# Tile addresses at multiples of 128 bytes, and three-pass products that run from the last column to the first

## The chip, the cores and the metric

The kernel runs on one core of one Trainium2 chip. The time is device microseconds of one execution of the whole program; the number used is the median of the runs shown. Names of engines: PE is TensorE (matrix products), PEld its weight load, DVE VectorE, ACT ScalarE, POOL GpSimd, SP the queue that issues most of the DMAs.

## What is computed

Two blocks of a model on 512 tokens of width 1024 (and 256 context tokens), all in float32. The matrix products that matter here are these, cut from the reference:

```python
z, xbc, dt_raw, q, f, v, g = _split(t @ w_in, IN_SIZES)            # first mixer, latent and context
...
return jnp.concatenate([ys, os_], axis=-1).astype(h.dtype) @ w_out
...
a, gate = jnp.split(t @ w1 + b1, 2, axis=-1)                       # conformer
u = dwconv1d(a * jax.nn.sigmoid(gate), dw_w, dw_b)
...
v, gate = jnp.split(t @ w_up, 2, axis=-1)                          # feed-forward, 1024 -> 2 x 2816
return (jax.nn.gelu(gate, approximate=False) * v) @ w_down         # 2816 -> 1024
...
proj = h @ w_in[l]                                                 # second block
x = x + jnp.concatenate([o_nsa, o_rw, o_moba], axis=-1) @ w_out[l]
x = x + _conv_glu(_rmsnorm(x, ffn_norm[l]), ffn_w_in[l], ...)
```

There are three feed-forward parts (two of the first block's form, one `_conv_glu`), and between them a chunked state-space scan, a gated linear recurrence, a 31-tap convolution, three kinds of attention and a delta-rule recurrence.

## The kernel before

Activations lie transposed: 128 features on the partitions, 512 tokens (256 for the context) along the row. A dense product walks over tiles of 128 output features; each tile is summed in one PSUM bank over the `kt` blocks of 128 input features (8, 22 or 16 of them).

For accuracy a float32 operand is split into two tiles of type float32r, a high and a low part, and each block is multiplied in three passes by the helper `three_passes`: weights high with activations high (line 248), weights high with activations low (line 249), weights low with activations high (line 250). Each pass is one MATMUL whose moving operand, the one that streams through the array, is a 512-column row of activations, and one LDWEIGHTS of 128 columns of weights. Nearly all dense layers call this helper. The value projection (lines 441 to 443) and a part of the second block's projections (lines 3676 to 3678) write out three passes of their own, in which the weights are the moving operand; the 31 taps of the convolution (line 1277) and the scans are plain float32 products.

Weights come in by DMA on SP, are split into high and low by ACT and DVE one or two tiles ahead, and lie in rotating slots. The feed-forward layers use four slots: two in `pre_high` and `pre_low`, which belong to the core's fixed arena, and two in the layer's own `ffn_w_high` and `ffn_w_low`. PE works through the tiles in the written order; what releases it is the split (`low_done`), and a free bank (`banks_free`).

Each tile is a tensor allocated by the helpers `room`, `split_room` and `some_parts` of the class `Core` on a stack from the low end of the memory or, with `side="right"`, from the high end. Its address is whatever the stack stands at. Every allocation has the same address on all partitions, and each row of a tile is a multiple of 512 bytes long for the operands named here, so that all rows of a tile have the tile's own residue to 128 bytes. The residues in the built program:

| moving tile | residue | weight tile | residue |
|---|---|---|---|
| ffn_x_high, ffn_x_low | 0 | ffn_w_high, ffn_w_low | 0 |
| ffn_x_high, ffn_x_low | 0 | pre_high, pre_low | 96 |
| ffn_h_high, ffn_h_low | 96 | ffn_down_w_high, _low | 32 |
| ffn_h, conf_x, conf_in, mix_parts, h | 96 | pre_high, pre_low | 96 |
| conf_x_high, conf_x_low | 96 | conf_w_high, conf_w_low | 96 |
| conf_in, mix_parts | 96 | conf_out_w, out_w | 0 |
| h_high, h_low, h_ctx | 96 | f_w, q_w, gate_w, pj_w | 32 |
| h_high, h_low, h_ctx | 96 | xbc_w | 0 |
| y, o | 32 | mix_out_w | 64 |
| y, o | 32 | mix_first | 32 |
| v_w (moving) | 32 | h, h_ctx (as weights) | 96 |

Of the kernel before, what the change touches and what calls it, by code (L numbers as in the profile page):

```python
# [8 lines left out]
F32 = mybir.dt.float32  # L9
F32R = mybir.dt.float32r  # L10
# [5 lines left out]
P = 128  # L16
# [50 lines left out]
ALWAYS = len(CONST)  # L67
# [63 lines left out]


ARENA = 28 * 1024


class Core:


    def __init__(self, nc, ctx):
        self.nc = nc  # L140
        self.stages = self.rooms = 0
        self.banks = [ctx.enter_context(nc.psum_tensor(f"bank{i}", [P, SEQ], F32)) for i in range(8)]
        self.const_sb = ctx.enter_context(nc.sbuf_tensor("const_sb", [P, ALWAYS, P], F32))
        self.some = {}
        self.cols_sb = ctx.enter_context(nc.sbuf_tensor("cols_sb", [P, N_COLS], F32))
        ctx.enter_context(nc.sbuf_tensor("arena", [P, ARENA // 4], F32, side="right"))
        self.arena_at = nc.sbuf_top
        slab = DT * P * 4
        self.pre_ring = self.in_arena("pre_ring", [P, 2, DT, P], F32, 0)
        self.pre_high = self.in_arena("pre_high", [P, 2, DT, P], F32R, 2 * slab)  # L150
        self.pre_low = self.in_arena("pre_low", [P, 2, DT, P], F32R, 4 * slab)
        self.rstd = self.in_arena("rstd", [P, SEQ], F32, 6 * slab)
        self.mean = self.in_arena("mean", [P, SEQ], F32, 6 * slab + SEQ * 4)
        self.fold_sb = ctx.enter_context(nc.sbuf_tensor("fold_sb", [P, 4, DEPTH * 2 - 1, DT], F32))
# [33 lines left out]
    @contextmanager  # L188
    def room(self, side=None, **shapes):

        self.rooms += 1
        n = self.rooms
        with ExitStack() as ctx:
            yield [ctx.enter_context(self.nc.sbuf_tensor(f"{name}_{n}", shape, F32, side=side)) for name, shape in shapes.items()]

    @contextmanager
    def split_room(self, side=None, **shapes):

        self.rooms += 1
        n = self.rooms  # L200
        with ExitStack() as ctx:
            yield [tuple(ctx.enter_context(self.nc.sbuf_tensor(f"{name}_{part}_{n}", shape, F32R, side=side))
                         for part in ("high", "low")) for name, shape in shapes.items()]

    @contextmanager
# [8 lines left out]
    @contextmanager  # L214
    def some_parts(self, **shapes):

        self.rooms += 1
        n = self.rooms
        with ExitStack() as ctx:
            yield [ctx.enter_context(self.nc.sbuf_tensor(f"{name}_{n}", shape, F32R)) for name, shape in shapes.items()]  # L220

    @contextmanager
    def stage(self, *names):
# [21 lines left out]
def three_passes(pe, bank, weights, acts, start, stop):  # L245


    pe.matmul(bank, weights[0], acts[0], start=start, stop=False)  # L248
    pe.matmul(bank, weights[0], acts[1], start=False, stop=False)  # L249
    return pe.matmul(bank, weights[1], acts[0], start=False, stop=stop)  # L250


def fill(pe, core, bank, count):
# [14 lines left out]
def gemm(core, name, weights, acts, spans, out, tiles, unroll, bias=None, func=ACT.Identity, more=None,  # L268
# [19 lines left out]
    with core.room(**{f"{name}_ring": [P, rings, kt, P]}) as (ring,), \  # L288
# [60 lines left out]
        @block.tensor  # L349
        def _(pe):  # L350
            pe.sem_inc(tile_done, slots)
            with pe.Fori(0, steps) as i:
                for u in range(unroll):

                    pe.wait_ge(banks_free, i * unroll + u + 1)
                    for n in range(len(spans)):
                        for k in range(kt):
                            if n == 0 and k in (0, kt // 2):
                                pe.wait_ge(low_done, 2 * (i * unroll + u) + (k > 0) + 1)
                            mm = three_passes(pe, bank(u, n), [part[:, u % slots, k, :] for part in (high, low)],  # L360
                                              taken(k, n), k == 0, k == kt - 1)
                    mm.then_inc(tile_done, 1)
# [196 lines left out]
def closing(core, name, weights, acts, x, gate=None, center=True, eps=EPS, ahead=0, nxt=None, source=None, feed=None, rest=None, sq=None, lead=None,  # L559
# [47 lines left out]
    with core.room(**rows) as (ring, shift, stat, eps_col, *own), \  # L607
# [45 lines left out]
        def _(pe):  # L653
# [10 lines left out]
            def product(u, k):  # L664
                t = units[u][0]
                mm = three_passes(pe, tile_bank(t), part(u, k), acts(k), k == 0, k == kt - 1)
                if k == units[u][2] - 1:
                    mm.then_inc(used, 1)
# [306 lines left out]
def glu_ffn(core, name, w_up, gate_at, value_at, w_down, make_feed, x, renew, width, interior, taps, middle, conv_w, conv_b, func,  # L975
# [14 lines left out]
    with core.split_room(**{f"{name}_h": [P, FT, SEQ]}) as (h,), \  # L990
            core.room(**{f"{name}_pad": [P, 2, width], f"{name}_acc": [P, 2, SEQ], f"{name}_val": [P, 2, SEQ],
                         f"{name}_lit": [P, 2, SEQ]}) as (pad, acc, val, lit):
        with core.split_room(**{f"{name}_x": [P, DT, SEQ], f"{name}_w": [P, 2, DT, P]}) as (parts, (high, low)):
# [3 lines left out]
            with core.stage(*names, *feed.names) as (block, *sems):  # L997
# [33 lines left out]
                @block.tensor  # L1031
                def _(pe):
                    def product(u, k):
                        weight = [part[:, k, :] for part in slot(u)]
                        return three_passes(pe, core.banks[u][:, :], weight, (parts[0][:, k, :], parts[1][:, k, :]), k == 0,
                                            k == DT - 1)

                    fill(pe, core, core.banks[4], 3)
                    for k in range(DT):
                        pe.wait_ge(fed, k + 1)  # L1040
                        for u in range(2):
                            mm = product(u, k)
                            if k == DT - 1:
                                mm.then_inc(tile_done, 1)
                    for u in range(2, 4):
                        pe.wait_ge(low_done, u + 1)
                        for k in range(DT):
                            mm = product(u, k)
                        mm.then_inc(tile_done, 1)
                    with pe.Fori(1, steps) as i:  # L1050
                        for u in range(4):
                            pe.wait_ge(low_done, 4 * i + u + 1)
                            pe.wait_ge(banks_free, 4 * i + u + 1)
                            for k in range(DT):
                                mm = product(u, k)
                            mm.then_inc(tile_done, 1)
# [542 lines left out]
class Folds:  # L1599
# [4 lines left out]
    def __init__(self, core, mods):  # L1604
        self.core, self.mods = core, mods
        self.gated_bias = core.in_arena("gated_bias", [P, DT], F32, ARENA - DT * 4)

# [2746 lines left out]
```

## Time and profile before

| | |
|---|---|
| time, median of three runs | 2832.42 us (2829.52 to 2840.2) |
| span of the profiled execution, first to last instruction | 2830.4 us |
| PE busy | 2644.2 us, 93% |
| PEld busy | 2033.9 us, 72% |
| DVE busy | 1646.7 us, 58% |
| ACT busy | 1091.3 us, 39% |
| three-pass products of the helper | 8304 MATMULs of 16080 |

The profiled execution has no time of its own outside its span in what is shown; its span stands 2.0 us under the median of the runs. A MATMUL's duration in the profile reaches from its start to its modelled end, and consecutive ones overlap; the time that one costs in a dense run is therefore the distance from its start to the start of the next.

### The profile page before, as it was taken

Reading aid. Unit: us, or ns where it says so; the run is one execution under the profiler, and the core shown is the slowest. Engines: PE = TensorE matmul, PEld = TensorE weight load, DVE = VectorE, ACT = ScalarE, POOL = GpSimd, SP = SyncE. Lnnn points to the kernel's source line nnn. Section 1 sums busy time; section 2 is a strip of 40 time slices with the busy share of each in tenths; the row PEclk is TensorE's granted clock in tenths of the full one; section 3 lists DMA queues with packets and bytes.
Section 4 is the critical chain, followed back from the end, with each engine's and each line's share of the span. In section 5 each row is a group of like instructions: output and inputs, shape, how many; then the busy total and the mean of one; then the engine's idle time right before and its main releaser. Section 6 shows DMA issues by size and latency. Waiting matters only on the chain. (4 is left out here: it accounts for less than half of the span.)

```text
span 2830.4 us, 41654 instructions
## 1 busy us (share of the span) xinstructions
PE 2644.2 (93%) x16080; PEld 2033.9 (72%) x16080; DVE 1646.7 (58%) x2595; ACT 1091.3 (39%) x1805; POOL 163.8 (6%) x170
## 2 busy tenths in 40 slices
PE   6978899988889999999999999999899998999998
PEld 3753588776678788877564688878588766788886
DVE  3436412267756587753798688853664676544432
ACT  3441210146553455522523465532322254355421
POOL 0005300013214000000000000000000000000000
PEclk9989999999989999999999999999999998999999
DMA  8734312211114133341211233342441001233231
GB/s 300 243 115 142 127 46 66 56 43 37 46 29 141 44 105 96 89 114 51 60 45 30 64 108 98 95 109 62 109 106 45 3 17 33 80 96 96 82 116 63
DMA packets 382115, 240.93 MB, mean 85 GB/s; under 512 B 7824, under 2 KB 353808, under 8 KB 381968
## 3 DMA queue, kind: packets, MB, share of 16 engines
q1 hardware_dynamic: 381968, 238.89, 28.9%
q8 instruction: 102, 1.67, 0.3%
q14 instruction: 45, 0.37, 0.0%
HBM read 236.24 MB, written 2.10 MB: 84 GB/s over the span
## 5 line engine op out<-in xcount | busy, mean ns | idle before, releaser
L1163 DVE SCALAR_TENSOR_TENSOR ffn_acc<-ffn_pad,cols_sb,ffn_acc 128x512 f32<-128x512 f32 x380 | 263.7, 746 | 31.3 <-ACT ffn_acc L1090 31.2
L248 PE MATMUL bank<-ffn_x_high,pre_high 128*128 128x512 f32 x528 | 210.9, 399 | 4.9 <-DVE ffn_x_low L479 3.3
L250 PE MATMUL bank<-ffn_x_high,pre_low 128*128 128x512 f32 x528 | 209.1, 396 | 0.0
L249 PE MATMUL bank<-ffn_x_low,pre_high 128*128 128x512 f32 x528 | 208.9, 396 | 0.0
L250 PE MATMUL bank<-ffn_x_high,ffn_w_low 128*128 128x512 f32 x528 | 205.5, 389 | 0.0
L248 PE MATMUL bank<-ffn_x_high,ffn_w_high 128*128 128x512 f32 x528 | 205.5, 389 | 0.0
L249 PE MATMUL bank<-ffn_x_low,ffn_w_high 128*128 128x512 f32 x528 | 205.4, 389 | 0.0
L248 PE MATMUL bank<-ffn_h_high,ffn_down_w_high 128*128 128x512 f32 x480 | 190.5, 397 | 1.5 <-DVE ffn_h_low L958 1.5
L249 PE MATMUL bank<-ffn_h_low,ffn_down_w_high 128*128 128x512 f32 x480 | 189.6, 395 | 0.0
L250 PE MATMUL bank<-ffn_h_high,ffn_down_w_low 128*128 128x512 f32 x480 | 188.6, 393 | 0.0
L753 ACT ACTIVATE ffn_down_w_high<-ffn_down_ring 128x1408 fp32r<-128x1408 f32 (+1 forms) x45 | 60.5, 1344 | 212.0 <-PE bank L250 176.9
L802 DVE TENSOR_TENSOR ffn_down_w_low<-ffn_down_ring,ffn_down_w_high 128x1408 fp32r<-128x1408 f32 (+1 forms) x45 | 71.2, 1581 | 112.0 <-ACT ffn_down_w_high L753 112.0
L1125 DVE TENSOR_TENSOR pre_low<-pre_ring,pre_high 128x1024 fp32r<-128x1024 f32 x60 | 73.4, 1223 | 98.1 <-ACT pre_high L1062 97.5
L248 PEld LDWEIGHTS bank<-ffn_x_high,pre_high 128*128 128x128 f32 x528 | 99.2, 188 | 36.0 <-DVE ffn_x_low L479 12.4
L1388 DVE SCALAR_TENSOR_TENSOR conf_u<-conf_pad,cols_sb,conf_u 128x512 f32<-128x512 f32 x156 | 117.3, 752 | 11.2 <-ACT conf_u L1354 5.5
L250 PEld LDWEIGHTS bank<-ffn_x_high,pre_low 128*128 128x128 f32 x528 | 99.2, 188 | 24.1
L249 PEld LDWEIGHTS bank<-ffn_x_low,pre_high 128*128 128x128 f32 x528 | 99.3, 188 | 23.5
L248 PEld LDWEIGHTS bank<-ffn_x_high,ffn_w_high 128*128 128x128 f32 x528 | 99.1, 188 | 20.9 <-DVE ffn_w_low L1125 0.2
L250 PEld LDWEIGHTS bank<-ffn_x_high,ffn_w_low 128*128 128x128 f32 x528 | 99.1, 188 | 20.7
L249 PEld LDWEIGHTS bank<-ffn_x_low,ffn_w_high 128*128 128x128 f32 x528 | 99.1, 188 | 20.6
L1125 DVE TENSOR_TENSOR ffn_w_low<-pre_ring,ffn_w_high 128x1024 fp32r<-128x1024 f32 x66 | 80.3, 1221 | 47.6 <-ACT ffn_w_high L1062 47.6
L248 PEld LDWEIGHTS bank<-ffn_h_high,ffn_down_w_high 128*128 128x128 f32 x480 | 90.2, 188 | 24.1 <-DVE ffn_h_low L958 2.4
(732 smaller groups left out, 6227.7 us busy)
## 6 DMA issues: line engine op xcount, KB each, us to landing
ada_ring<-in_ada_w SPq DMA_DIRECT2D x48, 1024.0 KB, 7.0
pre_ring<-in_ffn_w_up SPq DMA_DIRECT2D x88, 512.0 KB, 3.9
pre_ring<-in_ffn_w_in SPq DMA_DIRECT2D x44, 512.0 KB, 3.9
ffn_down_ring<-in_ffn_w_down SPq DMA_DIRECT2D x28, 704.0 KB, 4.6
pj_ring<-in_w_in SPq DMA_DIRECT2D x24, 512.0 KB, 4.0
ffn_down_ring<-in_ffn_w_out SPq DMA_DIRECT2D x14, 704.0 KB, 4.1
pre_ring<-in_conf_w SPq DMA_DIRECT2D x18, 512.0 KB, 4.8
f_ring<-in_mix_w_in SPq DMA_DIRECT2D x32, 256.0 KB, 3.2
```

Of the source, the lines that this page charges most:

```text
L248: pe.matmul(bank, weights[0], acts[0], start=start, stop=False)
L249: pe.matmul(bank, weights[0], acts[1], start=False, stop=False)
L250: return pe.matmul(bank, weights[1], acts[0], start=False, stop=stop)
L753: act.activation(high[n % slots][:, 0:k1 - k0], ring[:, n % 2, 0:k1 - k0], ACT.Copy).then_inc(piece_high, 1)
L802: dve.tensor_tensor(low[n % slots][:, 0:k1 - k0], ring[:, n % 2, 0:k1 - k0], high[n % slots][:, 0:k1 - k0].bitcast(F32), ALU.subtract).the ...
L1125: dve.tensor_tensor(slot(u)[1], ring[:, u % 2], slot(u)[0].bitcast(F32), ALU.subtract).then_inc(low_done, 1)
L1163: dve.scalar_tensor_tensor(out=dst, in0=src, scalar=conv_w(2 * i + j, n), in1=dst, op0=ALU.mult, op1=ALU.add).then_inc(tapped[j], 1)
L1388: dve.scalar_tensor_tensor(out=conv[:, j, :], in0=pad[:, j % pads, n:n + SEQ], scalar=core.col("conf_dw_w", j, n), in1=conv[:, j, :], op0= ...
```

## The change

It adds `align_bytes=LINE`, with LINE 128, to the allocations of the three helpers, of the constants and of the arena, and it turns the helper of the three passes round: the moving operand is read with a step of minus one from its last column, and the PSUM bank is written with a step of minus one from its last column, so that each result lands where it did. The weights are read as before.

```diff
+LINE = 128
...
-        self.const_sb = ctx.enter_context(nc.sbuf_tensor("const_sb", [P, ALWAYS, P], F32))
+        self.const_sb = ctx.enter_context(nc.sbuf_tensor("const_sb", [P, ALWAYS, P], F32, align_bytes=LINE))
...
-        ctx.enter_context(nc.sbuf_tensor("arena", [P, ARENA // 4], F32, side="right"))
+        ctx.enter_context(nc.sbuf_tensor("arena", [P, ARENA // 4], F32, side="right", align_bytes=LINE))
...
-            yield [ctx.enter_context(self.nc.sbuf_tensor(f"{name}_{n}", shape, F32, side=side)) for name, shape in shapes.items()]
+            yield [ctx.enter_context(self.nc.sbuf_tensor(f"{name}_{n}", shape, F32, side=side, align_bytes=LINE)) for name, shape in shapes.items()]
...
-            yield [tuple(ctx.enter_context(self.nc.sbuf_tensor(f"{name}_{part}_{n}", shape, F32R, side=side))
+            yield [tuple(ctx.enter_context(self.nc.sbuf_tensor(f"{name}_{part}_{n}", shape, F32R, side=side, align_bytes=LINE))
...
 def three_passes(pe, bank, weights, acts, start, stop):
 
 
-    pe.matmul(bank, weights[0], acts[0], start=start, stop=False)
-    pe.matmul(bank, weights[0], acts[1], start=False, stop=False)
-    return pe.matmul(bank, weights[1], acts[0], start=False, stop=stop)
+    back = bank[:, ::-1]
+    pe.matmul(back, weights[0], acts[0][:, ::-1], start=start, stop=False)
+    pe.matmul(back, weights[0], acts[1][:, ::-1], start=False, stop=False)
+    return pe.matmul(back, weights[1], acts[0][:, ::-1], start=False, stop=stop)
```

In the built program the instructions of every engine, their order and their waits are the same ones as before; they stand two lines lower in the file. What differs is the addresses, and the access patterns of the helper's MATMULs. Every tile of the table above now has the residue 0; every moving tile and its weights agree. The first operand of the first product reads `[[4096, 128], [1, 512]]` from element 0 before, and `[[4096, 128], [-1, 512]]` from element 511 now; its bank changes in the same way.

## Rows read from the trace of the kernel before

**Rows 1.** The page: busy time of each engine.
```profile
PE 2644.2 (93%) x16080; PEld 2033.9 (72%) x16080; DVE 1646.7 (58%) x2595; ACT 1091.3 (39%) x1805; POOL 163.8 (6%) x170
```

**Rows 2.** Windows of the span: length, busy time of each engine, granted clock, DMA.
```profile
600.00:800.00 200.00, 166.96 (x2193) 132.44 (x2192) 143.79 (x269) 118.96 (x230) 52.90 (x53) 0.91 0.16 42
1000.00:1300.00 300.00, 298.89 (x1292) 242.34 (x1291) 215.24 (x281) 138.77 (x179) 0.00 (x0) 1.00 0.36 101
1300.00:1600.00 300.00, 284.77 (x1034) 190.29 (x1033) 225.15 (x307) 112.73 (x196) 1.45 (x1) 0.98 0.16 45
2200.00:2400.00 200.00, 184.62 (x2647) 134.03 (x2643) 145.39 (x421) 85.48 (x245) 0.00 (x0) 0.92 0.05 12
2400.00:2831.00 431.00, 416.40 (x1818) 336.93 (x1816) 180.22 (x216) 171.97 (x223) 0.99 (x2) 0.99 0.31 90
```

**Rows 3.** Who waited for whom, PE's longest: us in total, times, longest.
```profile
PE bank L1568 <- DMA ada_ring<-in_ada_w: 24.6, 10, 7.8
PE bank L2435 <- DVE gs_k L2406: 11.1, 9, 5.5
PE bank L248 <- DVE q_w_low L265: 6.0, 1, 6.0
```

**Rows 4.** Windows of line 248 alone: PE's own, in two hundreds and in all.
```profile
600.00:800.00 200.00, 47.30 (x101) 19.94 (x101) 0.91 0.16 42
0.00:2831.00 2831.00, 1091.45 (x2768) 523.18 (x2768) 0.98 0.29 85
```

**Rows 5.** Timeline of PE: start and length in us. Feed-forward, the two kinds of slot.
```profile
1118.83 0.39 PE L248 MATMUL bank<-ffn_x_high,ffn_w_high 128*128 128x512 f32 x1
...
1124.27 0.39 PE L248 MATMUL bank<-ffn_x_high,pre_high 128*128 128x512 f32 x1
...
1129.88 0.40 PE L248 MATMUL bank<-ffn_x_high,pre_high 128*128 128x512 f32 x1
```

**Rows 6.** Timeline of PE, two more pairs of tiles.
```profile
1416.91 0.39 PE L248 MATMUL bank<-conf_x_high,conf_w_high 128*128 128x512 f32 x1
...
1419.63 0.39 PE L248 MATMUL bank<-conf_x_high,conf_w_high 128*128 128x512 f32 x1
...
1899.70 0.39 PE L248 MATMUL bank<-ffn_h_high,ffn_down_w_high 128*128 128x512 f32 x1
...
1901.10 0.39 PE L248 MATMUL bank<-ffn_h_high,ffn_down_w_high 128*128 128x512 f32 x1
```

**Rows 7.** Groups of PE instructions: count, busy us, mean ns of one, idle before.
```profile
L250 PE MATMUL bank<-ffn_x_high,pre_low 128*128 128x512 f32 x528 | 209.1, 396 | 0.0
L249 PE MATMUL bank<-ffn_x_low,pre_high 128*128 128x512 f32 x528 | 208.9, 396 | 0.0
L249 PE MATMUL bank<-ffn_x_low,ffn_w_high 128*128 128x512 f32 x528 | 205.4, 389 | 0.0
L248 PE MATMUL bank<-ffn_h_high,ffn_down_w_high 128*128 128x512 f32 x480 | 190.5, 397 | 1.5 <-DVE ffn_h_low L958 1.5
L249 PE MATMUL bank<-ffn_h_low,ffn_down_w_high 128*128 128x512 f32 x480 | 189.6, 395 | 0.0
L250 PE MATMUL bank<-ffn_h_high,ffn_down_w_low 128*128 128x512 f32 x480 | 188.6, 393 | 0.0
L250 PE MATMUL bank<-h_high,pj_w_low 128*128 128x512 f32 x144 | 56.4, 392 | 0.0
L249 PE MATMUL bank<-mix_parts_low,out_w_high 128*128 128x512 f32 x48 | 19.1, 399 | 0.0
L250 PE MATMUL bank<-ffn_h_high,pre_low 128*128 128x512 f32 x48 | 18.7, 390 | 0.0
L250 PE MATMUL bank<-h_ctx_high,f_w_low 128*128 128x256 f32 x128 | 35.8, 280 | 0.0
L442 PE MATMUL bank<-v_w_low,h_ctx_high 128*128 128x256 f32 x64 | 17.7, 276 | 0.0
```

**Rows 8.** Timeline of PE: the convolution's plain float32 products, back to back.
```profile
1399.06 4.88 PE L1277 MATMUL bank<-conf_pad,conf_diag 128*128 128x512 f32 x11
```

**Rows 9.** The convolution's group: count, busy us, mean ns of one.
```profile
L1277 PE MATMUL bank<-conf_pad,conf_diag 128*128 128x512 f32 x168 | 73.5, 592 | 1.5 <-DVE conf_u L1395 1.5
```

**Rows 10.** Timeline of the weight loads, at the first of rows 5.
```profile
1118.83 0.19 PEld L249 LDWEIGHTS bank<-ffn_x_low,ffn_w_high 128*128 128x128 f32 x1
1119.06 0.19 PEld L250 LDWEIGHTS bank<-ffn_x_high,ffn_w_low 128*128 128x128 f32 x1
```

More of the change, by code:

```diff
@@ L219, in some_parts @@
         with ExitStack() as ctx:
-            yield [ctx.enter_context(self.nc.sbuf_tensor(f"{name}_{n}", shape, F32R)) for name, shape in shapes.items()]
+            yield [ctx.enter_context(self.nc.sbuf_tensor(f"{name}_{n}", shape, F32R, align_bytes=LINE)) for name, shape in shapes.items()]
     @contextmanager
```

## The prediction, made before the changed kernel ran

> **What bounds the kernel now.** I read the page first: PE is busy 93% of the span, DVE 58%, ACT 39% [rows 1]. So the question is whether anything holds PE back where it is not busy, and what it does where it is. The windows answer by stage [rows 2]: from 1000 to 1300, in the feed-forward, PE has 298.89 of 300 us busy while DVE has 215.24 and ACT 138.77, and from 2400 on 416.40 of 431. The gaps lie elsewhere, at 600 to 800 (166.96 of 200) and 2200 to 2400 (184.62 of 200), in the recurrences. The waits [rows 3] are small and mostly there or at the start: 24.6 us for the first DMAs, 11.1 us for a recurrence, and single ones of 6 us for a split. The chain that ended last tells nothing, since it covers the last 10 us only. The kernel is bound by the rate at which PE takes the dense products, and line 248 and its two siblings are 3 x 2768 = 8304 of them [rows 4]. Of these 7656 have 512 columns and 648 have 256.
>
> That rate I took from starts, since the durations overlap. With ffn_x against ffn_w there are 24 MATMULs from 1118.83 to 1124.27: 226.7 ns each. With the same ffn_x against pre, 24 from 1124.27 to 1129.88: 233.8 ns [rows 5]. The clock, the shape and the order are the same; the operands differ in their addresses (residues 0 and 0, then 0 and 96). conf_x against conf_w, both at 96, is 12 in 2.72 us: 226.7 ns. ffn_h against ffn_down_w, 96 and 32, is 6 in 1.40 us: 233.3 ns [rows 6]. So what counts is not the residue 0 but that moving tile and weight tile agree. The mean durations say this for whole groups, being about 162 ns above the distance: 389 and 390 where residues agree, 392 to 399 where they do not [rows 7].
>
> The floor is lower than both. The plain float32 taps run back to back at (4.88 - 0.59) / 10 = 429 ns for 512 columns [rows 8, 9]. The 0.59 is one product's own length. At the full 2.4 GHz that is one column in two cycles; half of 429 is 214.5 ns, what 512 columns would take at one column per cycle. The helper's products lose 12.2 ns to that in the best case and 19 in the others.
>
> **The alignment.** It removes the disagreement everywhere. By the means [rows 7]: ffn_x against pre, 1584 MATMULs, 7 ns each (396 to 389), 11.1 us. ffn_h against ffn_down_w, 480 of each pass, 8 + 6 + 4 ns, 8.6 us. The other disagreeing pairs have 2160 MATMULs of 512 columns; their excess runs from 3 ns (pj, 392) to 10 ns (mix_parts low, 399). I count 4 ns, and leave out the 384 of the gate projection, most of which lie at 600 to 800 (line 248 has 101 products there [rows 4]), where PE is short of work in any case [rows 2]: 1776 x 4 ns = 7.1 us. With 256 columns, 280 against 276 ns, 640 x 4 ns = 2.6 us. Together 29.4 us. Were the pairing chance, this term would be nothing; but the four pairs timed [rows 5, 6] and the groups [rows 7] all point one way, so I keep it whole. The moved addresses cost nothing elsewhere: the instructions of the other engines are the same, and DVE and ACT have over 80 us of slack in the 300 of the feed-forward [rows 2].
>
> TensorE: Matmul & The Clock Gate, Part 2, step 1, of the Trainium skill says that PE has two independent SBUF read ports, so that the next tile's weight load does not slow the running product; by it this term would be 0 and alignment would be worth nothing. The trace disagrees, with 226.7 against 233.8 ns for one moving tile.
>
> **The reversal.** No product of the kernel before streams backwards, so its price is bounded. From below it is 214.5 ns per 512 columns, the half of the tap's distance. From above it is 429 ns, one column in two cycles, as for the taps [rows 8]. Within these the choice hangs on what the lost 12.2 ns are. A weight load starts with each product (1118.83 and 1118.83, 1119.05 and 1119.06 [rows 5, 10]), and the cost depends on how the two addresses stand to each other. So both reads touch something shared, and meet again and again. If the weights are fetched from the last column on, a forward moving tile runs against them and meets them often; a backward one runs with them and meets them seldom. If they are fetched forwards, turning one makes it worse. The trace does not show that direction. I take 220 ns, about the middle between the best case seen (226.7) and the floor (214.5), since one of the two streams stays twice as fast as the other and cannot avoid the other wholly. That is 6.7 ns on 7656 - 384 = 7272, 48.7 us, and half of it on 640 short ones, 2.1 us.
>
> **The sum.** 29.4 + 50.8 = 80.2 us of PE time. Nearly all of it lies in stretches where PE is the bound; I take 95%, for ends of stages, where a split or an eviction comes due earlier than it is done, and for DVE in the convolution (225.15 of 300 [rows 2]). That is 76 us: 2830.4 - 76 = 2754 for the profiled execution's span, and as that stood 2.0 us under the median, 2756 for the median. What comes due next is DVE's split of the weights: at 1000 to 1300 its share would go from 72% to 75%, still covered. A gain in the rate of 5% leaves the granted clock alone, which is 1.00 there already.
>
> **Rivals.**
> - *The reversal changes nothing in the rate; only the alignment pays.* For it: two forward tiles that agree are alike at 226.7 whatever their residue, so the 12.2 ns may be a fixed loss per stretch of columns. Against it: the taps have no such loss. 29.4 x 0.95 = 28 us: 2804.
> - *Backward streaming breaks the pairing of columns.* The 2.4 GHz rate may need two neighbouring columns per fetch or per write to the bank, in rising order; if not, one column takes two cycles, 429 ns. The place is every product of the helper: 7656 x (429 - 230) + 648 x (214 - 118) ns = 1524 + 62 us, so about 4420. For it: the plain float32 rows [rows 9] show that such a rate exists. Against it: the last two columns still share one aligned pair, both in the tile and in the bank. A hundredth of that price decides: the mean before is 230 ns (2448 products at 226.7, 5184 at 230 to 234), and from 232 ns on the time is over 0.5% above before, since 2 ns on 7272 are 14 us.
> - *The same shared thing, met more often.* The weights are fetched forwards, and every product falls to the rate of disagreeing pairs or a little worse, 234 to 238 ns: 7272 x 4 to 8 ns is 29 to 58 us, 2860 to 2890 at most, and about 2845 at the lower end, if only part does.
> - *Nothing moves at all*, since residue and direction were both mistaken for something else: 2832.
>
> On the second rival, Advanced Engine Details and Errata, PSUM Cachelines, of the Trainium skill says that these lines are 8 bytes, two float32 values, and that "Any non-contiguous AP significantly slows down matmuls". A step of minus one is either contiguous or not in that sense; the page doesn't say, and no row here shows it. By it the time would go to that rival's.
>
> **How the numbers follow.** Forecast (both terms pay) 0.45; alignment alone 0.22; met more often 0.10; broken pairs 0.20; nothing 0.03. What a measurement can tell from no change is about 0.5%, 14 us. Faster are the first two, 0.67; within 0.5% the last and half of "met more often", 0.08; slower the rest, 0.25. The forecast's own range goes from the floor, where (12.2 x 7272 + 6 x 640) ns + 29.4 us = 122 us, 95% of it 116 us, 2717, to 2785. The stated range goes from 2720 up to 2850, over the alignment alone and the lower end of "met more often"; broken pairs stay outside.
>
> **What would show it.** Start to start in the timeline of the changed kernel: ffn_x against pre as fast as against ffn_w shows the alignment. If both are near 220 the reversal pays; near 226.7 it is neutral; above 232 it costs; near 429 the pairs are broken, and the group's mean would be near 590 rather than 389. The convolution's 592 ns should not move, as the helper has no part in it. PE's busy share from 1000 to 1300 should stay at 99%; if it falls and DVE's or ACT's waits grow, the 95% were too much. The prediction is wrong by far only through the direction of the streams, which I could not read.

## The result and the profile after

The changed kernel took 2857.97 us (median of 4 runs) against 2832.65 us before. The ratio is 1.0089, with a 95% interval of 1.0074 to 1.0105: slower by 0.9%, some 25 us. 2756 us was forecast, with a range of 2720 to 2850. In the experiments each ratio is taken against runs of the kernel before made beside that run.

The page after, engines:

```profile
span 2859.2 us, 41654 instructions
PE 2679.2 (94%) x16080; PEld 2042.6 (71%) x16080; DVE 1647.4 (58%) x2595; ACT 1091.1 (38%) x1805; POOL 162.0 (6%) x170
```

PE is busy 35 us longer than in [rows 1]. The weight loads (PEld) take 9 us more; DVE, ACT and POOL are as they were. The window that answers to the second of [rows 2]:

```profile
1000.00:1300.00 300.00, 299.14 (x1280) 240.29 (x1280) 218.88 (x287) 138.86 (x179) 0.00 (x0) 1.00 0.35 101
```

It is just as full at the same clock, but holds 1280 products where it held 1292. PE doesn't wait more, it goes more slowly. The two longest waits of [rows 3] came back within 1 us:

```profile
PE bank L1570 <- DMA ada_ring<-in_ada_w: 23.7, 11, 7.5
PE bank L2437 <- DVE gs_k L2408: 10.9, 9, 5.5
```

The timeline of PE in the feed-forward, start and length in us, on both sides of the place where the two kinds of slot meet, as in [rows 5]:

```profile
1118.11 0.40 PE L250 MATMUL bank<-ffn_x_high,pre_high 128*128 128x512 f32 x1
...
1125.11 0.40 PE L250 MATMUL bank<-ffn_x_high,ffn_w_high 128*128 128x512 f32 x1
...
1130.71 0.40 PE L250 MATMUL bank<-ffn_x_high,ffn_w_high 128*128 128x512 f32 x1
```

From 1118.11 to 1125.11 there are 30 products, from 1125.11 to 1130.71 24: 233.3 ns each in both. The difference between the two slots is gone, and both stand where only the slower one stood. The groups of [rows 7] agree (mean ns of one):

```profile
L251 PE MATMUL bank<-ffn_x_low,pre_high 128*128 128x512 f32 x528 | 209.8, 397 | 0.0
L251 PE MATMUL bank<-ffn_x_low,ffn_w_high 128*128 128x512 f32 x528 | 209.8, 397 | 0.0
L251 PE MATMUL bank<-ffn_h_low,ffn_down_w_high 128*128 128x512 f32 x480 | 190.7, 397 | 0.0
L1279 PE MATMUL bank<-conf_pad,conf_diag 128*128 128x512 f32 x168 | 73.4, 592 | 0.0
```

Averaged over the helper's dense products of 512 columns (start to next start under 267 ns, 7315 before and 7318 after), the distance went from 230.6 to 233.6 ns. 3.0 ns on 7656 products are 23 us: nearly the whole loss of 25, and within its interval (21 to 30 us). Below, "the mean distance" is this figure for each kernel.

### The profile page after: what moved, and what is told of

Read it like the earlier page. It is cut to its first block and busy times, and to the rows that moved or that the text cites. A ratio compares the mean times of both kernels' runs of the same rounds, so it can differ in the third digit from the quotient of the medians.

```text
span 2859.2 us, 41654 instructions
## 1 busy us (share of the span) xinstructions
PE 2679.2 (94%) x16080; PEld 2042.6 (71%) x16080; DVE 1647.4 (58%) x2595; ACT 1091.1 (38%) x1805; POOL 162.0 (6%) x170
## 5 line engine op out<-in xcount | busy, mean ns | idle before, releaser
L804 DVE TENSOR_TENSOR ffn_down_w_low<-ffn_down_ring,ffn_down_w_high 128x1408 fp32r<-128x1408 f32 (+1 forms) x45 | 71.1, 1580 | 110.2 <-ACT ffn_down_w_high L755 110.2
```

The costliest lines, as they stand in the source:

```text
L804: dve.tensor_tensor(low[n % slots][:, 0:k1 - k0], ring[:, n % 2, 0:k1 - k0], high[n % slots][:, 0:k1 - k0].bitcast(F32), ALU.subtract).the ...
```

## The experiments

After the result I held **theory A**: the distance depends on whether the residues of moving tile and weight tile agree to 128 bytes, and the reversal did all the harm. **Theory B**: residues are a coincidence. **Theory C**: the alignment did the harm.

### Alignment alone

The changed kernel, with the three passes forward again:

```diff
-    back = bank[:, ::-1]
-    pe.matmul(back, weights[0], acts[0][:, ::-1], start=start, stop=False)
...
+    pe.matmul(bank, weights[0], acts[0], start=start, stop=False)
...
```

> The tiles at multiples of 128 bytes, the three passes forward as before. Theory A (the distance between products is set by whether moving tile and weight tile have the same residue to 128 bytes, and the reversal alone did the harm): every dense product of 512 columns at 226.7 ns, so about 28 us under the kernel before, 2804 us. Theory B (the residues are a coincidence; alignment does nothing): pairs keep their 227 to 234 ns, 2832 us. Theory C (alignment is what harmed): 2858 us, as the changed kernel.

Measured: 2827.43 us, ratio 0.998 (0.9965 to 0.9994). It is a gain, but a fifth of what theory A gave. The groups show why:

```profile
L250 PE MATMUL bank<-ffn_x_low,pre_high 128*128 128x512 f32 x528 | 207.3, 393 | 0.0
L250 PE MATMUL bank<-ffn_x_low,ffn_w_high 128*128 128x512 f32 x528 | 205.4, 389 | 0.0
L250 PE MATMUL bank<-h_low,pj_w_high 128*128 128x512 f32 x144 | 58.4, 405 | 0.0
L250 PE MATMUL bank<-ffn_h_low,pre_high 128*128 128x512 f32 x48 | 18.9, 395 | 0.0
L250 PE MATMUL bank<-mix_parts_low,out_w_high 128*128 128x512 f32 x48 | 18.7, 389 | 0.0
```

mix_parts against out_w went from 399 to 389, as it should. But ffn_x against pre stopped at 393, and ffn_h against pre, which agreed before and was fast (390), is now at 395, though all of these tiles are at multiples of 128. In the built program pre stands 128 bytes beyond a multiple of 256. The ffn_x of the first two feed-forward parts is at a multiple of 256; that of the third is 128 beyond one, as pre is. Every pair that I had counted as agreeing to 128 bytes before agreed to 256 as well. That makes **theory D**: the period is 256 bytes. This run's own timeline bears it out, with the same pair of names in the first feed-forward part and in the third:

```profile
1128.04 0.41 PE L249 MATMUL bank<-ffn_x_high,pre_high 128*128 128x512 f32 x1
...
1139.20 0.39 PE L249 MATMUL bank<-ffn_x_high,ffn_w_high 128*128 128x512 f32 x1
...
2519.89 0.39 PE L249 MATMUL bank<-ffn_x_high,pre_high 128*128 128x512 f32 x1
...
2530.77 0.39 PE L249 MATMUL bank<-ffn_x_high,ffn_w_high 128*128 128x512 f32 x1
```

Each stretch against pre is 48 products: 232.5 ns in the first, where the tiles stand 128 bytes apart, and 226.7 ns in the third, where they agree to 256. The mean distance is 229.1 ns; 1.5 ns on 7656 products would be 12 us, of which the measured time shows 6. These runs had a mean granted clock of 0.9729, the 17 of the kernel before beside them 0.9745, and within those 17 the runs at a lower clock tend to be the longer ones (2841.9 us at 0.966, 2826.9 at 0.979). The clock may have taken a part of the missing 6 us; that is not shown.

### Reversal alone

The kernel before, with the `[:, ::-1]` of the change only.

> The addresses of before, the three passes reversed. Theory A, if a reversed product costs 233.3 ns whatever the residues: 2858 us, as the changed kernel. Theory A, if a reversed product depends on the pair of residues as a forward one does, with another best pair: pairs of different residues differ from each other, and the time lies between 2840 and 2880 us. Theory C (alignment is what harmed): 2832 us or less.

Measured: 2855.98 us, ratio 1.0074 (1.0054 to 1.0094). All pairs are at 233.4 ns on average, whatever their residues:

```profile
L250 PE MATMUL bank<-ffn_x_low,ffn_w_high 128*128 128x512 f32 x528 | 209.8, 397 | 0.0
L250 PE MATMUL bank<-ffn_x_low,pre_high 128*128 128x512 f32 x528 | 209.4, 397 | 0.0
```

So the reversal carries the loss and theory C falls. Aligned to 128 bytes, in the changed kernel, a few small pairs are slower still (h against pj_w, conf_x and ffn_h against pre: 235 ns on average), the large ones the same.

### Rows of equal products, first set

The kernel before with a stage on PE ahead of the last one: rows of 48 products into bank 0, each row with its own line, on a buffer at a multiple of 128 bytes. `m(i, at)` is one of four moving rows, `w(i, at)` one of four weight tiles, `at` a shift in elements of 4 bytes.

```python
for i in range(48):
    pe.matmul(a[:, ::-1], w(i, 8), m(i)[:, ::-1], start=(i == 0), stop=(i == 47))
```

> The kernel before with 24 rows of 48 products each added on PE ahead of the last stage; each row repeats one form, four moving rows and four weight tiles in turn. Only the distance from start to start within a row is read. Theory A: forward products at 226.7 ns where both residues agree (0 and 0, 32 and 32) and 231 to 238 ns where they differ by 32, 64 or 96 bytes; reversed ones at 233.3 ns at 0 and 0. If only the read or only the write is reversed, the one that costs shows itself. If the loss comes from the weight load that runs beside the product, then products with 32 columns of weights lose less than 12 ns over 214.5, and a product of 256 columns loses as much as one of 512; if it is a fixed loss of the moving stream, 32 columns of weights change nothing and 256 columns lose half. Plain float32 should be 429 ns in either direction if the pairing of columns is not touched.

The timeline, a row of products in each line (start, length, count). The distance is the length less one product's own (0.39), divided by 47:

```profile
2867.97 11.36 PE L1538 MATMUL bank<-probe 128*128 128x512 f32 x48
...
2890.41 11.10 PE L1542 MATMUL bank<-probe 128*128 128x512 f32 x48
...
2912.55 11.37 PE L1546 MATMUL bank<-probe 128*128 128x512 f32 x48
...
2934.96 11.36 PE L1550 MATMUL bank<-probe 128*128 128x512 f32 x48
...
2957.36 11.36 PE L1554 MATMUL bank<-probe 128*128 128x512 f32 x48
2968.56 11.06 PE L1556 MATMUL bank<-probe 128*128 128x512 f32 x48
2979.45 11.28 PE L1558 MATMUL bank<-probe 128*32 128x512 f32 x48
...
3012.82 5.92 PE L1564 MATMUL bank<-probe 128*128 128x256 f32 x48
3018.58 5.85 PE L1566 MATMUL bank<-probe 128*128 128x256 f32 x48
3024.26 8.48 PE L1568 MATMUL bank<-probe 128*128 128x384 f32 x48
...
3079.14 41.36 PE L1574 MATMUL bank<-probe 128*128 128x512 f32 x96
...
3142.70 11.07 PE L1580 MATMUL bank<-probe 128*128 128x512 f32 x48
```

| line | form | ns |
|---|---|---|
| 1580, 1542 | forward, residues 0 and 0; 32 and 32 | 227 |
| 1538 | forward, weights 64 bytes further | 233 |
| 1546, 1550 | both reversed, weights at 0; 64 further | 233 |
| 1554 | only the read of the moving tile reversed | 233 |
| 1556 | only the write of the bank reversed | 227 |
| 1558 | forward, 32 columns of weights instead of 128 | 232 |
| 1568, 1564 | forward, 384 and 256 columns | 173, 120 |
| 1566 | both reversed, 256 columns | 118 |
| 1574 | plain float32, reversed: two MATMULs for each product | 429 each |

This settles four things. At 512 columns the backward **read** costs 6.6 ns; the backward write of the bank costs nothing. Reversed products don't care for the residue of the weights. The loss of a forward product over the full clock (213.3, 160 and 106.7 ns for 512, 384 and 256 columns) is 13.3 ns in each, so it seems to belong to the product, not to its columns. And narrower weights don't take it away: with 32 columns of weights the loss is 18 ns, though these tiles agree. That speaks against a plain meeting of two reads during the weight load, as I had pictured it. At 256 columns the backward read costs nothing (118 against 120 ns), so its price is no fixed amount for each product.

The row of plain float32 also corrects my floor's wording. Its 48 products left 96 MATMULs, and the convolution's 84 products left the 168 of [rows 9]: a plain product is two of them, 2 x 429 = 859 ns for 512 columns, which is four times 214.7 ns. The figure of the floor, 214.5 ns for 512 columns, stays the same.

### Addresses at multiples of 256 bytes

`LINE = 256`, forward and reversed.

> As the run with alignment alone, but with addresses at multiples of 256 bytes. Theory D (moving tile and weight tile must have the same residue to 256 bytes, not to 128; rounding to 128 bytes repaired some pairs and broke others): every dense forward product of 512 columns near 226.7 ns, among them ffn_x and conf_x against pre, ffn_h against pre and h against pj_w, which were 230 to 233 ns with 128 bytes; 230.6 to 227 ns over 7300 products is 26 us, 2806 us. Theory A with 128 bytes as the period: as with 128 bytes, 2827 us.

> The changed kernel with 256 for 128 bytes, the three passes reversed. If a reversed product costs 233.3 ns whatever the residues: about 2856 us, as the changed kernel. If a reversed product needs the residues to 256 bytes to agree before it shows a gain: under 2832 us.

Forward: 2807.63 us, ratio 0.9923 (0.9907 to 0.994). Reversed: 2854.02 us, ratio 1.0087 (1.0071 to 1.0103). The timeline of the forward one, where the slots change:

```profile
1119.17 0.39 PE L249 MATMUL bank<-ffn_x_high,ffn_w_high 128*128 128x512 f32 x1
...
1124.61 0.39 PE L249 MATMUL bank<-ffn_x_high,pre_high 128*128 128x512 f32 x1
...
1130.05 0.39 PE L249 MATMUL bank<-ffn_x_high,pre_high 128*128 128x512 f32 x1
```

24 products in 5.44 us on either side: 226.7 ns for both kinds of slot. The group of ffn_x against pre went down with it:

```profile
L250 PE MATMUL bank<-ffn_x_low,pre_high 128*128 128x512 f32 x528 | 205.6, 389 | 0.0
```

The mean distance is 227.3 ns forward and 233.4 reversed. Theory D holds, and the forward kernel is faster than the kernel before and the changed one.

### Rows of equal products, second set

> Again rows of 48 equal products ahead of the last stage. Theory D: forward with the weights 256 bytes further 226.7 ns, with the weights 128 or 384 bytes further, or the moving tile 128 bytes further, 230 to 240 ns; both 128 bytes further 226.7. Reversed rows 233.3 ns at all residues. If the loss is a fixed amount for each product: 496, 480 and 448 columns lose the same 13.3 ns over 2.4 GHz as 512, and 256. If the reversed loss comes from the backward steps, then eight pieces of 64 columns, each read backwards, cost as much as a full reversal and pieces taken in backward order but read forwards cost as a forward product; if it comes from where a row ends and the next begins, it is the other way round. The same weights or the same moving tile again and again should change nothing.

```profile
2858.72 11.32 PE L1536 MATMUL bank<-probe 128*128 128x512 f32 x48
2869.87 11.05 PE L1538 MATMUL bank<-probe 128*128 128x512 f32 x48
2880.76 11.32 PE L1540 MATMUL bank<-probe 128*128 128x512 f32 x48
...
2903.06 11.04 PE L1544 MATMUL bank<-probe 128*128 128x512 f32 x48
...
2979.99 9.89 PE L1558 MATMUL bank<-probe 128*128 128x448 f32 x48
2989.72 10.07 PE L1560 MATMUL bank<-probe 128*128 128x448 f32 x48
...
3011.07 5.62 PE L1566 MATMUL bank<-probe 128*128 128x256 f32 x48
...
3038.68 11.05 PE L1572 MATMUL bank<-probe 128*128 128x512 f32 x48
3049.57 11.37 PE L1574 MATMUL bank<-probe 128*128 128x512 f32 x48
3060.77 11.06 PE L1576 MATMUL bank<-probe 128*128 128x512 f32 x48
```

Weights 128, 256 and 384 bytes further (lines 1536, 1538, 1540): 232, 227, 232 ns; both tiles 128 bytes further (1544): 227. The period is 256 bytes. Eight pieces of 64 columns, each read backwards (1574): 233 ns, as for a whole row. The same pieces in backward order but read forwards (1576), or two halves so (1572): 227. The cost lies in the step of minus one, not in where a row begins. 448 columns (1558, own length 0.365) take 203 ns, a loss of 16 ns; 480 and 496 columns lose 17, not 13.3 as I expected, so the loss is not exactly fixed. 448 columns reversed (1560) take 207 ns: the backward read costs 6.6 ns at 512 columns, 4 at 448 and nothing at 256. A reversed row whose moving tile starts 4 bytes further takes 235.6 ns. With 256 columns and the weights 64 bytes further (1566, own length 0.276) a product takes 114 ns, less than the 120 of agreeing tiles: for the short products agreement is not the best.

### Pieces in backward order, in the whole kernel

```diff
+    pieces = lambda a: a.rearrange("p (h t) -> p h t", h=8)[:, ::-1, :]
+    back = pieces(bank)
+    pe.matmul(back, weights[0], pieces(acts[0]), start=start, stop=False)
...
```

> The kernel with addresses at multiples of 256 bytes, its three passes taken in eight pieces from the last piece to the first, each piece read and written forwards. If the cost of the reversal lies in the backward step from column to column: as the forward kernel with 256 bytes, 2807 us, 226.7 ns a product. If it lies in starting at the far end of a row: as the changed kernel, about 2855 us.

Measured: 2806.61 us, ratio 0.9909 (0.9891 to 0.9928), mean distance 227.3 ns. As the forward kernel with 256 bytes, within the intervals.

### The weight slots in the arena moved

```diff
-        ctx.enter_context(nc.sbuf_tensor("arena", [P, ARENA // 4], F32, side="right", align_bytes=LINE))
-        self.arena_at = nc.sbuf_top
+        ctx.enter_context(nc.sbuf_tensor("arena", [P, ARENA // 4 + 8], F32, side="right", align_bytes=LINE))
+        self.arena_at = nc.sbuf_top + 32
```

> The forward kernel with 256 bytes, but the arena, and with it the weight slots pre_high and pre_low, moved by 32 bytes; nothing else moves. Theory D: the 2064 products whose weights lie in pre fall from 226.7 to 233.3 ns, 6.6 ns each, 13.6 us: 2821 us; ffn_x against ffn_w stays at 226.7. If the residues are no cause: 2807 us.

Measured: 2818.8 us, ratio 0.9954 (0.9939 to 0.9969).

```profile
L250 PE MATMUL bank<-ffn_x_low,pre_high 128*128 128x512 f32 x528 | 208.8, 395 | 0.0
L250 PE MATMUL bank<-ffn_x_low,ffn_w_high 128*128 128x512 f32 x528 | 205.5, 389 | 0.0
```

ffn_x against pre went up from 389 to 395, and so did the other products whose weights lie in pre (conf_x and ffn_h against it: 233 ns from start to start); ffn_x against ffn_w stayed. The other tiles of the arena moved too, none of them an operand of these products. The address is a cause, not a companion, and theory B falls. The difference in ratio to the forward kernel, 0.0031 or 9 us, is under the 13.6 us worked out, but within what the two intervals allow.

## Why the prediction was wrong

**What bounds the kernel** was right. All seven whole kernels differ by the rate of the dense products. The mean distance times 7656, against the kernel before, gives +23, -12, +21, -26, +21, -25 and -13 us for the changed kernel, alignment alone, reversal alone, 256 bytes forward, 256 bytes reversed, pieces and the moved arena. The ratios gave +25, -6, +21, -22, +25, -26 and -13. Little was given back to DVE or ACT. In one run only, alignment alone, does the worked out figure (-12) lie outside the measured interval (-10 to -2 us); what takes the rest was not found.

**The alignment**, 29.4 us of PE time: the mechanism was right, the period wrong. "What counts is not the residue 0 but that moving tile and weight tile agree" holds, but to 256 bytes. The agreeing pairs before agreed to both, so the trace could not tell the two; I took the number that stood in the diff. Rounding to 128 mended some pairs, left ffn_x against pre 128 bytes apart in two of three parts, and broke others (conf_x, conf_in, mix_parts and ffn_h against pre, h against pj_w), and it measured 6 us. At 256 bytes the same term measured 22 us (17 to 26), under the 28 on the path. The 2.6 us for 256 columns in it had no ground: the row taken as agreeing, v_w against h_ctx at 276 ns, has residues 32 and 96. With tiles that agree to 256 bytes, h_ctx against f_w went up from 118 to 120 ns.

**The reversal**, 50.8 us of gain: this step failed, and it decided the sign. I set 220 ns "about the middle between the best case seen (226.7) and the floor (214.5)". Measured: 233.3 ns, 6.6 above the best case instead of 6.7 below it. The ground for it was the picture of two reads meeting while the weights load, with one stream "twice as fast as the other", a ratio that no row shows. The rows with 32 columns of weights (232 ns, not less than 227) speak against it, and the reversed rows, which ignore the weights' address, speak against a relative direction. The 2.1 us for 256 columns in the term did not come either: h_ctx against f_w takes 118 ns before and after. The floor itself was no guide: no form of a 512-column product in these rows came under 226.7 ns, so a value below the best row seen was the hope of the picture alone.

**The rivals**: "the same shared thing, met more often" came nearest: it put the rate at 234 to 238 ns and the time at 2845 to 2890, but got 0.10. Its reason, that the weights are fetched forwards, was not shown. The rule of the Trainium skill on PSUM lines (Advanced Engine Details and Errata, PSUM Cachelines), with the rival of broken pairs, didn't come in: with the bank alone written backwards a product takes 227 ns, the same as forwards. The other rule (TensorE: Matmul & The Clock Gate, Part 2, step 1), that a weight load does not slow the running product, gave the alignment nothing; the run with the arena moved is against that, with the group's mean up from 389 to 395 ns.

Why 256 bytes, and why at 512 columns a backward read costs the same 6.6 ns as many of the disagreeing addresses, stays open. Both land on 233.3 ns on average, which is 560 cycles of 2.4 GHz, where the good case is 544. Nor do residues fix the price of a disagreement: in the kernel before, h against f_w and h against q_w stand at the same addresses, weights 64 bytes under the moving tile, and take 228.9 and 233.3 ns. No row of equal products tried that difference.

## What to carry to other kernels

Where float32r products are dense, look at the distance from start to start by pair of tiles, not at the mean; a difference of 3% between pairs of the same shape was an address here, and came back by placing moving and weight tiles at one residue to 256 bytes (0.8% of this kernel). An address rule read from pairs that happen to exist should be tried with its double before it is built in. A stream direction that no row shows is not to be priced below the best row seen: take the rate of the nearest bad row as the likelier case, and try it in a row of 48 products first.

## What the runs showed of the hardware

- A float32r product of 512 columns with 128 columns of weights takes 226.7 ns at 2.4 GHz where moving and weight tile agree to 256 bytes. Where they don't, rows of equal products take 232 to 234 ns on average, their single distances 228 to 241 ns; pairs of the whole kernel take 229 to 234. With agreeing tiles but 32 columns of weights it takes 232 ns.
- A backward read of the moving tile takes 233.3 ns at 512 columns, at every residue of the weights tried (0, 32, 64, 96, 128 and 256 bytes), and 235.6 with the moving tile 4 bytes further. At 448 columns it costs 4 ns, at 256 nothing. A backward write of the bank is free.
- The loss against the full clock is 13.3 ns for 256, 384 and 512 columns, and 16 to 17 for 448, 480 and 496. 256 columns with tiles 64 bytes apart lose only 7 (113.7 ns).
- A plain float32 product of 512 columns is two MATMULs of 429 ns, forward and backward; the direction does not touch it.
